# Order of the work in one recurrent layer: a later sum of squares, unused products at two idle places, earlier RWKV inputs, splits ahead of stores

## The reference, cut to what matters

```python
h = rmsnorm(x, norm_pre_mix)
z = h @ w_in                        # 2048 x P_TOTAL, its columns are shared out to:
#   A: RG-LRU    B: gated MLP (layernorm of gelu(v), product along the sequence)
#   C: RWKV-7    D: mLSTM with 4 heads    and 4 gate blocks
y_a, y_b, y_c, y_d = rglru(..), gmlp(..), rwkv7(..), mlstm(..)
m = sum_b sigmoid(z_gate_b) * (y_b @ w_branch[b])
x = x + rmsnorm(m @ w_out, norm_post_mix)
hf = rmsnorm(x, norm_pre_ffn)
g, u = split(hf @ w_ff_in)
x = x + rmsnorm((silu(g) * u) @ w_ff_out, norm_post_ffn)
```

## Time and profile before

| | us |
|---|---|
| three timed runs | 2124.4, 2125.14, 2126.0 (median 2125.14) |
| profiled execution, its own time | 2118.58 |
| its span | 2116.8 |
| mean granted TensorE clock | 0.99 |
| median landing of a 512 KB piece of `w_in` after its issue | 3.9 |

### The profile page before, as it was taken

How to read it: one execution, slowest core, us unless ns; L and a number is a source line. 1 busy time by engine, 2 the same in 40 slices (tenths; PEclk the granted TensorE clock), 3 DMA queues, 4 the chain that set the end, 5 groups by cost and what they waited for, 6 DMA issues and landing times.

```text
span 2116.8 us, 39764 instructions
## 1 busy us (share of the span) xinstructions
PE 2067.8 (98%) x15855; PEld 2026.7 (96%) x15855; DVE 706.9 (33%) x1123; ACT 766.0 (36%) x942; POOL 1442.9 (68%) x1104
## 2 busy tenths in 40 slices
PE   7999999999999999999999999999999999999997
PEld 7999998898999999899999999999999999999997
DVE  5568444567432222637511711111000111111112
ACT  5354332434422222333333633333333333333332
POOL 6777754557765554579877677777777677777774
PEclk9999999999999999999999999999999999999998
DMA  7655645554544443368564454545545444454552
GB/s 242 195 183 186 199 141 163 171 162 151 166 149 130 126 130 117 116 216 275 190 208 149 130 150 148 149 149 149 150 145 155 150 146 150 145 157 138 153 153 98
DMA packets 122487, 337.47 MB, mean 159 GB/s; under 512 B 14328, under 2 KB 49508, under 8 KB 122000
## 3 DMA queue, kind: packets, MB, share of 16 engines
q1 hardware_dynamic: 104896, 313.98, 48.5%
q10 hardware_dynamic: 17488, 22.02, 2.9%
HBM read 312.07 MB, written 23.88 MB: 159 GB/s over the span
## 4 chain that ended last, share of the span: by engine, by line
PE 54%; POOL 24%; issue 21%; DVE 1%; POOLq 0%; ACT 0%; DVEq 0%
POOL w_lo L1457 24%; PE banks_g L1488 16%; PE banks_g L1487 16%; PE banks_g L1486 16%; PE banks_g L1593 1%; PE banks_g L1594 1%; PE banks_m L1594 1%; PE banks_m L1593 1%; PE banks_g L1595 1%; PE banks_m L1595 1%; PE banks_g L1619 0%; PE banks_g L1620 0%; PE banks_g L1623 0%; PE banks_m L1486 0%; PE banks_m L1488 0%
## 5 line engine op out<-in xcount | busy, mean ns | idle before, releaser
L1457 POOL TENSOR_TENSOR w_lo<-w_raw,w_hi 128x512 fp32r<-128x512 f32 (+1 forms) x1096 | 1436.5, 1335 | 652.8 <-ACT w_hi L1868 316.1
L1486 PE MATMUL banks_g<-x_hi,w_hi 128*128 128x320 f32 x3200 | 1004.5, 314 | 7.2 <-POOL w_lo L1457 6.9
L1488 PE MATMUL banks_g<-x_hi,w_lo 128*128 128x320 f32 x3200 | 991.5, 310 | 0.0
L1487 PE MATMUL banks_g<-x_lo,w_hi 128*128 128x320 f32 x3200 | 991.3, 310 | 0.0
L1486 PEld LDWEIGHTS banks_g<-x_hi,w_hi 128*128 128x128 f32 x3200 | 603.4, 189 | 17.9 <-issue 7.6
L1487 PEld LDWEIGHTS banks_g<-x_lo,w_hi 128*128 128x128 f32 x3200 | 603.7, 189 | 1.6
L1488 PEld LDWEIGHTS banks_g<-x_hi,w_lo 128*128 128x128 f32 x3200 | 603.4, 189 | 0.0
L1868 ACT ACTIVATE w_hi<-w_raw 128x1024 fp32r<-128x1024 f32 x188 | 197.1, 1057 | 428.7 <-PE banks_g L1488 363.9
L1763 ACT ACTIVATE w_hi<-w_raw 128x1024 fp32r<-128x1024 f32 (+1 forms) x248 | 258.0, 1041 | 244.7 <-PE banks_g L1488 242.6
L1488 PE MATMUL banks_g<-a_hi,w_lo 128*128 128x320 f32 x704 | 217.4, 309 | 0.0
L1486 PE MATMUL banks_g<-a_hi,w_hi 128*128 128x320 f32 x704 | 217.4, 309 | 0.0
(11 more groups left out here) (372 smaller groups left out, 1759.7 us busy)
## 6 DMA issues: line engine op xcount, KB each, us to landing
w_raw<-in_w_f SPq DMA_DIRECT2D x211, 512.0 KB, 3.9
w_raw<-in_w_fi SPq DMA_DIRECT2D x176, 512.0 KB, 3.7
w_raw<-in_w_fo SPq DMA_DIRECT2D x64, 512.0 KB, 3.5
front_scratch<-ev ACTq DMA_DIRECT2D x106, 160.0 KB, 2.4
w_raw<-in_w_br SPq DMA_DIRECT2D x32, 512.0 KB, 4.8
w_raw<-in_w_o SPq DMA_DIRECT2D x32, 512.0 KB, 3.7
arena<-front_scratch SPq DMA_DIRECT2D x24, 640.0 KB, 5.9
w_raw<-in_w_fo SPq DMA_DIRECT2D x32, 384.0 KB, 3.1
```

Source lines behind the costliest of these rows:

```text
L1457: low = nc.gpsimd.tensor_tensor(w_lo[:, q % RING, c0:c1], w_raw[:, q % RING, c0:c1], w_hi[:, q % RING, c0:c1].bitcast(F32), ALU.subtract)
L1486: pe.matmul(out, wh, hi[:, k0 + k, :], start=first and k == 0, stop=False)
L1487: pe.matmul(out, wh, lo[:, k0 + k, :], start=False, stop=False)
L1488: mm = pe.matmul(out, wl, hi[:, k0 + k, :], start=False, stop=last and k == tiles - 1)
```

## The change

1. **Start.** TensorE does nine unused products (`idle_products`) from a tile of constants into M[3] while it waits for the first weights. ScalarE splits two further pieces ahead of the root.
2. **Sum of squares.** It comes after piece 7, not after piece 5. Blocks 4 and 5 go to the banks M[2] and M[3] (`SPARE`), blocks 6 and 7 to G as before, and VectorE reads them there.
3. **gMLP.** "B_in" has six pieces, not five. VectorE does its evacuations up to "B_v" ahead of its wait for the gelu.
4. **ScalarE.** `full` on ScalarE now also makes one split beyond the count (`ahead`) before it waits for the bank, and within its front work the split for two further levels stands ahead of a store, at most up to the level wanted.
5. **RWKV inputs.** SyncE loads `c_low` and `c_gd` within head 3 of the mLSTM; `c_d`, the tile for the difference to the row before, has another place in `arena`; VectorE waits for `D_out` only after r, k and v are mixed. The wait for `c_lora` and `c_g2` is now on TensorE, ahead of their products.
6. **Feed-forward start.** TensorE does 14 unused products from the first high weights into G[3] while it waits for `x_hi`.

```diff
--- before.py
+++ after.py
@@ -244,7 +244,7 @@
         h_turned = arena[:, 10 * 256:13 * 256].rearrange("p (h e) -> p h e", e=64)
-        c_d = vc.take(4, T)
+        c_d = arena[:, 1414:1414 + 4 * T].rearrange("p (a b) -> p a b", a=4)
         c_d96 = arena[0:96, 0:T]
@@ -340,10 +340,13 @@
         part = {}
+        ahead = {}
...
             part[eng](at[key])
+            if eng in ahead:
+                ahead[eng](at[key] + 1)
             b, i = plan[key]
@@ -411,7 +414,7 @@
-            fill("B_in", 5)
+            fill("B_in", 6)
             pe.wait_ge(S("B_added"), 1)
@@ -525,6 +528,7 @@
             pe.wait_ge(S("C_low"), 2)
+            pe.wait_ge(S("C_lora_in"), 32)
             for h in hs:
@@ -771,6 +775,13 @@
                     sp.dma_start(d_wk, a["ml_wk"][h + 1]).then_inc(S("D_wq_in"), 16)
+                if h == 3:
+                    part[sp](at[("D_sb", h)] + AFTER)
+                    for name in ("D_Mb", "D_eb", "D_sb"):
+                        was_read(sp, name, h)
+                    sp.dma_start(c_low, zD[ZB["low"]][0:64, :]).then_inc(S("C_low_in"), 16)
+                    stored(sp, ZB["gd"])
+                    sp.dma_start(c_gd, zD[ZB["gd"]][0:96, :]).then_inc(S("C_gd_in"), 16)
                 after("D_Cp", h)
@@ -786,9 +797,6 @@
             sp.wait_ge(S("D_out"), 128)
-            sp.dma_start(c_low, zD[ZB["low"]][0:64, :]).then_inc(S("C_low_in"), 16)
-            stored(sp, ZB["gd"])
-            sp.dma_start(c_gd, zD[ZB["gd"]][0:96, :]).then_inc(S("C_gd_in"), 16)
             sp.dma_start(c_lora, a["rw_lora"]).then_inc(S("C_lora_in"), 16)
@@ -883,7 +891,6 @@
             act.wait_ge(S("C_mixed_low"), 1)
-            act.wait_ge(S("C_lora_in"), 32)
             sc.activation(c_low[0:32, :], c_low[0:32, :], ACT.Tanh).then_inc(S("C_low"), 1)
@@ -1032,6 +1039,7 @@
                 ts(b_v[:, c, :], b_v[:, c, :], V("ln_g", c), V("ln_b", c), ALU.mult, ALU.add).then_inc(S("B_v"), 1)
+            upto(dve, "B_v")
             dve.wait_ge(S("B_gelu_u"), 1)
@@ -1190,7 +1198,6 @@
             vb4 = lambda name: bc(V(name, 0, 4), 2, T)
-            dve.wait_ge(S("D_out"), 128)
             dve.wait_ge(S("C_sh_in"), 48)
@@ -1207,6 +1214,7 @@
                     put(tt(c_rk, c_kk, c_kk, ALU.mult), "C_kk_sq", 1)
+            dve.wait_ge(S("D_out"), 128)
             for h in range(4):
@@ -1388,6 +1396,7 @@
         LEAD = 16
+        SPARE = {4: 2, 5: 3}
@@ -1537,8 +1546,14 @@
+            def idle_products(lhs, rhs, out, n):
+                for _ in range(n):
+                    pe.matmul(out[:, 0:T], lhs, rhs, start=True, stop=True)
+
             for b in range(4):
                 pe.wait_ge(S(f"evac{b}"), 1)
+            pe.wait_ge(S("dve_order"), 1)
+            idle_products(small[:, 0:P], small[:, 0:T], M[3], 9)
             pe.wait_ge(S("w_hi_made"), 1)
@@ -1558,10 +1573,16 @@
                 mm.then_inc(S("w_used"), 1)
-                if p == 5:
-                    pe.wait_ge(S("con_in"), 16)
-                    sum_squares("x")
-            front_turns(8, LEAD // 8 - 1)
+            pe.wait_ge(S("con_in"), 16)
+            sum_squares("x")
+            for block in range(4, LEAD // 2):
+                p, b = 2 * block, block % 4
+                if block in SPARE:
+                    for half in range(2):
+                        products(p + half, (p + half) % RING, SPARE[block], 8, x_hi, x_lo, 8 * half, half == 0, half == 1,
+                                 banks=M)
+                else:
+                    front_block(block // 4, b, p)
             front_done = [LEAD]
@@ -1609,6 +1630,8 @@
                         pe.wait_ge(S(f"evac{b}"), use_ff[0][b] + 1)
+                    pe.wait_ge(S("w_lo_made"), FF0 + (RING + 1))
+                    idle_products(w_hi[:, 0, 0:P], w_hi[:, 0, 0:T], G[3], 14)
                     for p in range(8):
@@ -1823,6 +1846,8 @@
             first_split(8)
+            first_split(9)
+            first_split(10)
             root("x")
@@ -1850,7 +1875,7 @@
-            for p in range(6, LEAD):
+            for p in range(8, LEAD):
                 first_split(p + AHEAD)
@@ -1870,12 +1895,13 @@
                 for p in range(front_done[0], level):
-                    front_split(p + 1)
+                    front_split(min(p + 2, level))
                     if p % 2:
...
             part[act] = front_act
+            ahead[act] = front_split
             mixers_act(act, front_split)
@@ -2039,11 +2065,12 @@
-            def front_evac(use, b, p):
+            def front_evac(use, b, p, bank=None):
...
                 dve.wait_ge(S(f"ev_out{b}"), use * 16 + 16)
-                v.tensor_tensor(ev[:, b, :], G[b][:, 0:T], rstd[:, :], ALU.mult).then_inc(S(f"evac{b}"), 1)
+                v.tensor_tensor(ev[:, b, :], (G[b] if bank is None else bank)[:, 0:T], rstd[:, :],
+                                ALU.mult).then_inc(S(f"evac{b}"), 1)
@@ -2052,7 +2079,8 @@
             for block in range(LEAD // 2):
-                front_evac(block // 4, block % 4, 2 * block + 1 if block >= 4 else 6 + block // 2)
+                front_evac(block // 4, block % 4, 2 * block + 1 if block >= 4 else 6 + block // 2,
+                           M[SPARE[block]] if block in SPARE else None)
             front_done = [LEAD]
...
             def front_dve(level):
```

## The result

| | before | changed |
|---|---|---|
| median of four runs | 2124.77 us (2123.17 to 2126.0) | 2138.41 us (2136.14 to 2141.55) |
| profiled execution, its own time | 2118.58 us | 2141.55 us |
| its span | 2116.8 us | 2139.8 us |

The ratio is 1.007 (95% interval 1.0058 to 1.0083): slower by 13.6 us in the medians, where 2124.5 (2115 to 2132) was predicted. The two profiled executions lie further apart, 23.0 us: that of before is 6.2 under its median, that of after 3.1 above. So a difference between these two traces says where time goes, and runs say how much.

A forecast was written before the change was run, and what follows sets the result against it. TensorE, busy 98% of the span, was taken as the bound, with only idle places and slow-clock stretches to win. Terms summed to -0.6 us, 2118.0 for the profiled execution; 2124.5 was predicted for timed runs, range 2115 to 2132.

The forecast's parts named there:

- The start: First weights: unused products keep the clock warm, so piece 0 runs faster; -0.2 us, bounds -0.4 and +1.5.
- The sum of squares: Front start: with the sum later and two blocks in spare banks, block 4 starts at 39.6; -6.2 us, bounds -6.4 and -5.
- B_sum's wait: gMLP: the sixth piece in B_in covers TensorE's 3.1 us wait; -3.1 us.
- B_turned: gMLP: the extra split delays the variance's root, so TensorE waits up to 3.2 us for the normalised v; +2.5 us.
- the heads: mLSTM heads: ScalarE's copies wait for one more loaded piece, +10.3 us (3.2 to 14); new slow-clock stretches, +2.0 (0 to +5).
- `c_lora`'s order: RWKV inputs loaded earlier: TensorE's 2.6 us starvation near 470 and the half-clock stretch behind it go; -4.4 us.
- The end: Front part's end: "end" becomes piece 212, so RWKV's y loses its cover by pieces; +5.2 us, bounds +3.4 and +7.
- The second idle place: Feed-forward start: fourteen unused products may keep the clock, but VectorE's sum limits the gain; -0.7 us, bounds -0.8 and +0.3.
- Rival (b): mLSTM heads 1 to 3: copies wait for loads to the upper bound, a slow stretch after each; 2131 us, chance 0.22.
- my own signs: Line 470's waits in the heads: 12 to 16 us in all if right; 4 us or over 19 if wrong.
- splits ahead of stores: RWKV near 510: one split more before a store covers TensorE's 4.3 us wait and slow stretch; -6.0 us, bounds -6.0 and -4.5.
- the clock: Granted clock halves behind idle places; stretches of 7.0, 8.0 and 5.0 us read as 3.4, 3.4 and 1.7 us lost.

The follow-up runs named there:

- e8: The e4 kernel (changed kernel, no extra split, END_MORE 7) without the nine and the fourteen unused products: 2112.25 us.
- e1: The changed kernel without the extra split in `full` on ScalarE, all else kept: 2117.48 us, ratio 0.9974 to before.
- e2: The changed kernel with END_MORE 7 in place of 8, so eight front pieces follow RWKV's y: 2134.64 us, ratio 1.005 to before.
- e12: The changed kernel with RWKV's r, k and v loaded behind the heads' weight pieces and next w_q and w_k: 2133.64 us, ratio 1.0051 to before.
- e4: The changed kernel without the extra split in `full` on ScalarE and with END_MORE 7: 2111.48 us, ratio 0.994 to before.
- e9: The e4 kernel with ScalarE's old order in its front work, one split and then the store: 2107.63 us, ratio 0.9927 to before.

## Why the prediction was wrong

The first rows of TensorE in the changed kernel answer to the earlier trace rows:

```profile
2.45 7.15 PE L1551 MATMUL banks_m<-small 128*128 128x320 f32 x18 [2.45 <-PEq L1483]
9.20 1.57 PE L1547 MATMUL banks_g<-x_hi,w_hi 128*128 128x320 f32 x8
...
14.28 0.42 PE L1547 MATMUL banks_g<-x_hi,w_hi 128*128 128x320 f32 x1 [1.16 <-POOL w_lo L1466]
```

**Right in mechanism.** The start (-0.2): the unused products end at 9.2, piece 0's first eight products take 1.57 us where they took 2.47, and piece 1 begins at 14.28 behind GpSimd, against 14.36 before. (Without the unused products, in e8, it began at 13.79, so that no gain can be told.) The sum of squares: 6.2 us ahead at the gates when alone, as its term of -6.2 says; but the run with it alone is only 0.8 us faster. B_sum's wait is gone. The wait that moved to B_turned and the copies of the heads were named as the place of the loss. `c_lora`'s order: -4.6 in the trace where -4.4 was put. The end: 4.39 us ahead of line 1614, +5.7 in the trace for +5.2, although no line of the diff is there; in the medians its removal gave 3.8. The second idle place (-0.7) gave 0.1: the slow stretch is gone, but TensorE then waits 0.53 us for VectorE's sum. The Sigmoid of head 2 again started 1.29 us after its table load, without a further drain.

**Mis-sized: the heads, +10.3 and +2.0.** The table gives 21 in place of 12.3. Of these, 15.6 go when the extra split is taken out (e1). The waits rose by 14.1 us (18.4 - 4.3) in place of 10.3: head 1 waited 5.8 us for 5.2 forecast, head 2 6.9 for 6.2, head 3 5.8 for 3.2. The term that was too small is the landing. I took 1.6 us for a further piece at full queue rate, and none in head 3, of which I said that nothing big was between; in the trace the pieces that the heads want land 6.4 to 7.6 us behind their issue, with three or four other large transfers issued beside them, and head 3 had the state's load and SyncE's wait for the outputs like the others. The other 7 us of the 21 fit the time at half clock, 34 us in the heads where it was 7; I had put one or two stretches more. Of this part some 4 us stay in e1, without the long waits, so it isn't all a price of the waits.

Rival (b) had the mechanism, the copies waiting for loads to the upper bound, at a chance of 0.22. By my own signs the case was not even decided: 18.4 us at the line that was 470 lies over the 12 to 16 of the sum and just under the 19 of (b). And its price, 2131, was 7 us short as well.

**Mis-sized: B_turned, +2.5.** It waited 5.1 us, and the slow stretch behind it cost 2.9 more in the table, so 8.2 in all. I had no clock term here, though my own upper figure was 3.2 us, and in the trace of before all but one (that ahead of B_sum) of the waits of 2 us or more are followed by a slow stretch. The size of this wait varies: it was 5.1, 4.6 and 3.7 us in the traces of the changed kernel, e2 and e12, which don't differ up to there.

**Failed: splits ahead of stores, -6.0.** I followed ScalarE through one stage only. A split that stands earlier changes all the places where ScalarE works ahead of a store: it costs 7 us alone, and 3.9 within e4. The 6.1 us in RWKV were won, but mostly by the shift of one piece: that shift alone left 1.2 of the 4.3 us, the split order alone 4.3. That this part of the sum came out at -6.1 in the trace is luck.

**Missing: the RG-LRU and 268.** Two waits of 2.1 and 2.2 us, one with a slow stretch, are in no term. Both came from the split order (both are in the run with it alone, and neither in e9).

**Read too high: the clock.** I took the length of a stretch at half clock as time in which TensorE works. In the first of the earlier trace rows it was busy for 5.11 of 7.00 us, so that 2.5 us and not 3.4 were lost there.

In medians: removing the extra split is worth 20.9, the split order costs 3.9 within e4, and "end" 3.8. The terms of the extra split (2.5, 10.3 and 2.0) were put at 14.8, that of the split order at -6.0; with these two measured values the sum would have been -0.6 + 6.1 + 9.9 = +15.4, against 13.6. That it comes so near is in part luck: it leaves out what the shift won near 510, that "end" cost 3.8 and not 5.2, and that the later sum of squares was worth 0.8 and not 6.2 alone.

The range was too narrow on the slow side because its upper end was one rival's price, with the other terms held at their middle.

## What to carry to other kernels

Work done ahead by an in-order engine is only free when its input is already there: put it behind the small step that another engine waits for, or count the landing of that input as measured in the same crowded stretch. When a helper is changed, go through every place that calls it, and see with whom the work that now starts earlier will collide. And where a planner fills up to a multiple, work out its counts again after any shift.

## What was not expected of the hardware

VectorE's operation on 128 x 64 took 1.32 us beside a GpSimd operation and 0.27 without, that on 128 x 256 1.52 and 0.47. The granted clock fell to half in the mLSTM heads behind no wait over 0.5 us (at 303 and 409 in the changed kernel), in some kernels and not in others. And TensorE waited 5.3 us without a releaser at line 577, among hundreds of 64 x 64 products, in one kernel, and 1.5 to 3.8 in others with the same work there.
